# Dense feed-forward with 128-token blocks as the stationary operand of all three products, gate and up weights side by side, and the inner layer transposed on TensorE

## The chip, the cores and the metric

The program runs on one core of one Trainium2 chip. TensorE (PE) multiplies: a 128x128 stationary operand is loaded and up to 512 columns of the moving operand are streamed past it into a bank of PSUM. ScalarE (ACT), VectorE (DVE) and GpSimd (POOL) compute on data in SBUF, and ACT and DVE read PSUM too; SyncE (SP) issues the loads. The metric is the device time of one execution in microseconds.

## The reference

A ten-stage stack on 256 tokens of width 1024: mixers (latent attention and RWKV-7, Mamba-2, LRU with window attention, gated DeltaNet), two cross attentions, three dense feed-forward layers and one mixture of experts. The change touches the three dense layers. Each computes, with 2816 inner columns:

```python
def swiglu_ffn(h, norm, w13, w2):
    u = rms_norm(h, norm) @ w13
    return (jax.nn.silu(u[..., :FFN_HIDDEN]) * u[..., FFN_HIDDEN:]) @ w2
```

The third layer has gate, up and down weights as three tensors instead of two. The result is added to `h`. All inputs are float32.

## The kernel before, in words

The stages follow one another in one instruction program; `swiglu` writes the three dense stages ffn0, ffn1 and ffn2. Each engine has its own in-order program, and semaphores (`wait_ge`, `then_inc`) tie them. Every product is taken in three passes (`passes`, lines 194 to 196): each operand is a rounded high part and a remainder (low part), and high x high, low x high and high x low are added up in PSUM. ACT makes the high part of a weight by a cast, DVE the low part by a subtraction, and the low part is written over the raw weights in the ring.

The inner columns are worked off in 11 chunks of 256. A chunk's weights are 3 MB: gate (128 x 8 x 256 per partition view), up (the same) and down (128 x 2 x 1024); two buffers of 6144 columns, `units`, `low` and `high`, alternate. A chunk is two steps j of 128 inner columns, 22 steps in all.

- `up(i, first, j)` on PE: the weights are stationary (128 inner columns), the 256 tokens move. 2 (gate, up) x 8 (k) x 3 passes = 48 matmuls of 256 columns. The inner layer so comes out transposed, inner columns on partitions, as the down product needs it. Four banks, one for each step of two chunks.
- ACT applies Silu (L2102), DVE multiplies (L2133), ACT casts (L2104), DVE takes the remainder (L2135).
- `down(i, j)` on PE, two steps behind `up`: the transposed inner layer is stationary, 512 weight columns move. 2 (t) x 2 (n) x 3 passes = 12 matmuls of 512 columns into four banks `acc` that collect over the whole stage.

PE's order is up 0, up 1, up 2, down 0, up 3, down 1, and so on to up 21, down 19, down 20, down 21. SP loads gate and up of a chunk when the up steps of the chunk before the last are done (`up_columns`), and down when that buffer's down steps are done. ACT casts a chunk's gate and up (L2090) ahead of the Silu of the chunk before, and its down weights (L2108) after its own second step; DVE follows (L2118, L2138). The first and the last bodies of the loop are written out; the middle is a hardware loop over two chunks. In front of the stage the tokens are normalised and transposed (`norm_rows`, `transpose_split`, L355, L369, L382).

The expert stage, `experts_by_tile`, is not touched. In it 128 rows are stationary and 512 weight columns move in all three products (also in three passes), and its inner layer is turned on PE by four transposes (L2460) once per 72 matmuls.

## Time and profile before

| | |
|---|---|
| median of 3 runs | 3296.67 us |
| the runs | 3291.42, 3296.67, 3301.78 us |
| span of the profiled execution | 3301.1 us |
| PE / weight loads / DVE / ACT busy | 83% / 69% / 57% / 42% |
| ffn0 | first matmul of `up` 677.7, first of the four additions to `h` 871.8 us |
| ffn1 | 1288.6 to 1482.7 us |
| ffn2 | 1665.1 to 1858.6 us |

The profiled execution's own time beside its span is not listed apart; the highest of the three runs, 3301.78 us, lies 0.7 us over the span. Times of the trace are microseconds from the span's start. The three dense stages take some 194 us each, 18% of the span together.

### The profile page before, as it was taken

To read this page: it belongs to the slowest core of one execution; us is meant where nothing else is said; L and a number is where in the kernel's file an instruction comes from. 1 tells how busy PE (TensorE), PEld (TensorE's weight loads), DVE (VectorE), ACT (ScalarE), POOL (GpSimd) and SP (SyncE) were. 2 spreads that over 40 slices of the span, in tenths; PEclk is the share of its full clock that TensorE was granted. 3 is DMA by queue.
4 is the path that set the end of the run, shared out by engine and by line. 5 is a ranking of instruction groups with operands and counts; after the bars stand their busy time and mean duration, and the time that the engine had idled before them with its cause. 6 is when DMAs were issued, how large, how long until landed. Compare 5 with 4: busy or idle time off the path is not lost.

```text
span 3301.1 us, 38219 instructions
## 1 busy us (share of the span) xinstructions
PE 2755.3 (83%) x14374; PEld 2282.4 (69%) x14374; DVE 1880.5 (57%) x2337; ACT 1397.5 (42%) x1812; POOL 328.7 (10%) x197
## 2 busy tenths in 40 slices
PE   7036876789899877997889896757999999999999
PEld 6023765489787746985589785756877877877877
DVE  3054224354484524544354474347888888888887
ACT  3012111144353304432244351115776777777766
POOL 3020111000144400000000132220000000000000
PEclk9565777889897698998699897877999999999999
DMA  7330001055452113534055440006999999999996
GB/s 178 74 119 0 1 1 38 13 182 187 157 175 78 40 63 109 184 132 139 1 196 181 157 143 0 1 0 258 386 342 330 370 323 330 376 321 341 362 325 227
DMA packets 334486, 564.59 MB, mean 171 GB/s; under 512 B 60274, under 2 KB 139122, under 8 KB 334256
## 3 DMA queue, kind: packets, MB, share of 16 engines
q1 hardware_dynamic: 333552, 559.52, 48.5%
q0 software_dynamic: 544, 1.84, 0.2%
q8 instruction: 70, 1.15, 0.1%
q10 hardware_dynamic: 288, 1.83, 0.1%
q14 instruction: 32, 0.26, 0.0%
HBM read 560.27 MB, written 1.05 MB: 170 GB/s over the span
## 4 chain that ended last, share of the span: by engine, by line
PE 76%; DVE 10%; ACT 5%; SPq 3%; issue 2%; POOL 2%; DMA 1%; ACTq 0%; DVEq 0%; POOLq 0%
PE banks L194 18%; PE banks L196 17%; PE banks L195 17%; PE banks L452 5%; SPq L263 3%; PE banks L844 1%; PE banks L868 1%; PE banks L869 1%; POOL arena L393 1%; PE banks L2395 1%; DMA ring<-in_mla_w_uq 1%; PE banks L1771 1%; PE banks L704 1%; PE banks L2460 1%; ACT arena L854 1%
## 5 line engine op out<-in xcount | busy, mean ns | idle before, releaser
L2541 DVE TENSOR_TENSOR moe_weights_low<-ring,moe_weights_high 128x1024 fp32r<-128x1024 f32 x672 | 784.4, 1220 | 118.3 <-ACT moe_weights_high L2495 113.1
L2495 ACT CAST moe_weights_high<-ring 128x1024 fp32r<-128x1024 f32 x672 | 684.0, 1052 | 127.8 <-PE banks L196 123.1
L194 PE MATMUL banks<-moe_weights_high,moe_rows_high 128*128 128x512 f32 x896 | 357.6, 399 | 3.7 <-DVE moe_weights_low L2541 3.7
L196 PE MATMUL banks<-moe_weights_low,moe_rows_high 128*128 128x512 f32 x896 | 350.6, 391 | 0.0
L195 PE MATMUL banks<-moe_weights_high,moe_rows_low 128*128 128x512 f32 x896 | 349.9, 390 | 0.0
L194 PE MATMUL banks<-ffn_x_high,ffn_weights_high 128*128 128x256 f32 x1056 | 300.5, 285 | 15.4 <-DVE ring_low L2118 15.4
L195 PE MATMUL banks<-ffn_x_high,ring_low 128*128 128x256 f32 x1056 | 300.0, 284 | 0.0
L196 PE MATMUL banks<-ffn_x_low,ffn_weights_high 128*128 128x256 f32 x1056 | 299.5, 284 | 0.0
L2118 DVE TENSOR_TENSOR ring_low<-ring,ffn_weights_high 128x2048 fp32r<-128x2048 f32 x66 | 148.1, 2289 | 134.7 <-ACT ffn_weights_high L2090 134.7
L194 PEld LDWEIGHTS banks<-ffn_x_high,ffn_weights_high 128*128 128x128 f32 x1056 | 203.0, 192 | 18.9 <-issue 16.5
L195 PEld LDWEIGHTS banks<-ffn_x_high,ring_low 128*128 128x128 f32 x1056 | 202.3, 192 | 2.4
L196 PEld LDWEIGHTS banks<-ffn_x_low,ffn_weights_high 128*128 128x128 f32 x1056 | 202.7, 192 | 0.0
L194 PEld LDWEIGHTS banks<-moe_weights_high,moe_rows_high 128*128 128x128 f32 x896 | 169.0, 189 | 39.0 <-issue 5.5
L196 PEld LDWEIGHTS banks<-moe_weights_low,moe_rows_high 128*128 128x128 f32 x896 | 168.7, 188 | 36.2
L195 PEld LDWEIGHTS banks<-moe_weights_high,moe_rows_low 128*128 128x128 f32 x896 | 169.2, 189 | 35.5 <-issue 1.7
L487 POOL TENSOR_TENSOR ring_low<-ring,pieces_high 128x1024 fp32r<-128x1024 f32 (+2 forms) x63 | 169.0, 2695 | 219.0 <-ACT pieces_high L473 218.9
L194 PE MATMUL banks<-moe_weights_high,moe_hidden_high 128*128 128x512 f32 x448 | 176.7, 394 | 11.7 <-DVE moe_hidden_low L2553 11.7
L2090 ACT CAST ffn_weights_high<-ring 128x2048 fp32r<-128x2048 f32 x66 | 122.3, 1901 | 144.5 <-DMA ring<-in_ffn_w 64.8
L452 PE MATMUL banks<-ring,arena 128*128 128x512 f32 (+1 forms) x296 | 134.3, 615 | 52.7 <-DMA ring<-in_mla_w_uq 42.5
L196 PE MATMUL banks<-moe_weights_low,moe_hidden_high 128*128 128x512 f32 x448 | 174.6, 390 | 0.0
L195 PE MATMUL banks<-moe_weights_high,moe_hidden_low 128*128 128x512 f32 x448 | 174.4, 389 | 0.0
L393 POOL TENSOR_TENSOR arena<-arena,consts 128x2 f32<-128x2 f32 (+3 forms) x34 | 44.1, 1298 | 1115.6 <-DVE arena L414 786.0
(482 smaller groups left out, 5275.1 us busy)
## 6 DMA issues: line engine op xcount, KB each, us to landing
ring<-in_o_moe_w_gate SPq DMA_DIRECT2D x112, 1024.0 KB, 6.7
ring<-in_o_moe_w_up SPq DMA_DIRECT2D x112, 1024.0 KB, 7.3
ring<-in_o_moe_w_down SPq DMA_DIRECT2D x112, 1024.0 KB, 6.6
ring<-in_ffn_w SPq DMA_DIRECT2D x66, 1024.0 KB, 7.8
ring<-in_od_w_in SPq DMA_DIRECT2D x10, 2048.0 KB, 7.9
ring<-in_o_w_in SPq DMA_DIRECT2D x8, 2048.0 KB, 8.8
ring<-in_e_ffn_w_gate SPq DMA_DIRECT2D x11, 1024.0 KB, 5.4
ring<-in_e_ffn_w_up SPq DMA_DIRECT2D x11, 1024.0 KB, 7.9
```

Source lines behind the costliest of these rows:

```text
L194: pe.matmul(out_, lh, rh, start=start, stop=False)
L195: pe.matmul(out_, ll, rh, start=False, stop=False)
L196: return pe.matmul(out_, lh, rl, start=False, stop=stop)
L263: sp.dma_start(dst, src, allow_slow_non_contiguous=True).then_inc(self.sem, 16)
L393: pool.tensor_tensor(x, x, const("minus_half")[:, 0:n], ALU.pow).then_inc(*G.tick())
L452: last = pe.matmul(bank.ap[:, 0:n], lhs[0:rows, k, t * P:(t + 1) * P], view[:, k, :], start=(k == 0), stop=(k == n_k - 1))
L487: pool.tensor_tensor(low_view, view, high.bitcast(F32), ALU.subtract).then_inc(*G.tick())
L704: last = pe.matmul(bank.ap[:, t * T:(t + 1) * T], b["qk"][0:d, t * P:(t + 1) * P], b["qk"][0:d, T:2 * T], start=True, stop=True)
L2090: act.copy(high[b][:, c], units[b][:, c]).then_inc(up_high, 1)
L2118: dve.tensor_tensor(low[b][:, c], units[b][:, c], high[b][:, c].bitcast(F32), ALU.subtract).then_inc(up_low, 1)
L2495: act.copy(hi[:, b * 1024:(b + 1) * 1024], piece).then_inc(sems["hi_done"], 1)
L2541: dve.tensor_tensor(lo[:, b], piece, hi[:, b].bitcast(F32), ALU.subtract).then_inc(sems["lo_done"], 1)
```

## The change

The tokens become stationary in the gate and up products too. The gate and up weights of a chunk lie side by side, so that one matmul moves 512 columns (256 of gate, 256 of up): `up(i, first, b)` now does a whole chunk, 2 (token block t) x 8 (k) x 3 passes = 48 matmuls of 512 columns, in two banks. The inner layer then has tokens on partitions; `turn` transposes it by four 128x128 transposes into a third bank, ACT casts out of that bank (`hidden`, 512 wide) and DVE takes the remainder. `down(i, b)` does 24 matmuls of 512 columns, a chunk at a time and one chunk behind. The PE order is up 0, turn 0, up 1, down 0, turn 1, up 2, down 1, and so on to up 10, down 9, turn 10, down 10. SP loads down 0 ahead of gate and up of chunk 1. `transpose` is the same call that other stages use with `ident`.

```diff
             enter(stage)
-            sg = [room(T) for _ in range(4)]
-            hid = [room(T) for _ in range(4)]
-            hh, hl = ([split_room(f"{stage}_hidden{j}_{part}", T) for j in range(4)] for part in ("high", "low"))
+            FC = 2 * P
+            sg = [room(FC) for _ in range(TT)]
+            hid = [room(FC) for _ in range(TT)]
+            hh, hl = split_room(f"{stage}_hidden_high", TT * FC), split_room(f"{stage}_hidden_low", TT * FC)
             xh, xl = (split_room(f"{stage}_x_{part}", KD * T).rearrange("p (k t) -> p k t", t=T)
...
             normed = transpose_split(scaled, KD, scaled_ready, xh, xl, g, par.landed())
             high = [split_room(f"{stage}_weights{b}_high", UNIT) for b in range(2)]
...
-            up_banks, acc = banks[0:4], banks[4:8]
+            UP, HALF_UP = KD * 2 * FC, KD * FC
+            up_view = lambda u: u[:, 0:UP].rearrange("p (k n) -> p k n", n=2 * FC)
+            down_view = lambda u: u[:, UP:UNIT].rearrange("p (k n) -> p k n", n=D)
+            up_banks, turn_bank, acc = banks[0:2], banks[2], banks[4:8]
...
-                body(steps // 4, False, 2)
+                assert chunks % 2 == 1
+                body(0, True, 2)
+                with eng.Fori(1, chunks // 2) as i:
+                    body(i, False, 2)
+                body(chunks // 2, False, 1)
...
+                def load_up(b, c):
+                    w = up_view(units[b])
+                    sp.dma_start(w[:, :, 0:FC], src("gate", c).rearrange("(k p) n -> p k n", p=P)).then_inc(up_landed[b], 16)
+                    sp.dma_start(w[:, :, FC:2 * FC], src("up", c).rearrange("(k p) n -> p k n", p=P)).then_inc(up_landed[b], 16)
+
+                def load_down(b, c):
+                    sp.dma_start(down_view(units[b]), src("down", c).rearrange("(k p) n -> p k n", p=P)).then_inc(down_landed[b], 16)
...
+                def body(i, first, count):
+
+                    for b in range(count):
+                        c = i * (2 * FC) + b * FC
                         sp.wait_ge(up_done, i * 4 + (2 * b - 2))
-                    sp.dma_start(wg[b], src("gate", c).rearrange("(k p) n -> p k n", p=P)).then_inc(up_landed[b], 16)
-                    sp.dma_start(wu[b], src("up", c).rearrange("(k p) n -> p k n", p=P)).then_inc(up_landed[b], 16)
-
-                def body(i, first, count):
-                    for b in range(count // 2):
-                        if count == 4:
-                            up_columns(i + b, 1 - b)
-                        c = i * (4 * P) + b * (2 * P)
-                        if not first:
-                            sp.wait_ge(down_done, i * 4 + (2 * b - 2))
...
+                        load_up(b, c)
+                        if not (first and b == 0):
+                            sp.wait_ge(down_done, i * 2 + (b - 2))
+                        load_down(1 - b, c - FC)
+                load_up(0, 0)
+                load_down(0, 0)
+                load_up(1, FC)
+                body(1, True, 2)
+                with sp.Fori(2, chunks // 2) as i:
+                    body(i, False, 2)
+                body(chunks // 2, False, 1)
+                sp.wait_ge(down_done, chunks - 2)
+                load_down((chunks - 1) % 2, (chunks - 1) * FC)
...
-                def up(i, first, j):
-                    b = j // 2
-                    if not first:
-                        pe.wait_ge(product_done, i * 4 + (j - 3))
-                    ps = up_banks[j].ap
-                    for which, w in enumerate((gate_w, up_w)):
-                        if j % 2 == 0:
-                            pe.wait_ge(up_low, i * 4 + (j + which + 1))
+                def up(i, first, b):
+                    wh, wl = up_view(high[b]), up_view(low[b])
+                    for t in range(TT):
+                        if not (first and b == 0):
+                            pe.wait_ge(product_done, i * 4 + (2 * b + t - 1))
+                        tok = slice(t * P, (t + 1) * P)
                         for k in range(KD):
-                            c = slice((j % 2) * P, (j % 2 + 1) * P)
-                            wh, wl = w[b]
-                            last = passes(pe, ps[:, which * T:(which + 1) * T], (wh[:, k, c], wl[:, k, c]),
-                                          (xh[:, k, :], xl[:, k, :]), start=(k == 0), stop=(k == KD - 1))
-                    last.then_inc(up_done, 1)
...
-                            last = passes(pe, acc[t * 2 + n].ap, (hh[j][:, rows], hl[j][:, rows]),
-                                          tuple(w[:, j % 2, cols] for w in down_w[b]), start=start, stop=stop)
+                            if t == 0 and k % (KD // 2) == 0:
+                                pe.wait_ge(up_low, i * 4 + (2 * b + k // (KD // 2) + 1))
+                            last = passes(pe, up_banks[t].ap, (xh[:, k, tok], xl[:, k, tok]), (wh[:, k, :], wl[:, k, :]),
+                                          start=(k == 0), stop=(k == KD - 1))
+                        last.then_inc(up_done, 1)
+
+                def turn(i, b):
+
+                    pe.wait_ge(product_done, i * 4 + (2 * b + 2))
+                    for j in range(2):
+                        for t in range(TT):
+                            at = j * T + t * P
+                            last = pe.transpose(turn_bank.ap[:, at:at + P], hid[t][:, j * P:(j + 1) * P], ident)
+                    last.then_inc(turn_done, 1)
+
+                def down(i, b, start=False, stop=False):
+                    pe.wait_ge(down_low, i * 2 + (b + 1))
+                    pe.wait_ge(hl_done, i * 2 + (b + 1))
+                    wh, wl = down_view(high[b]), down_view(low[b])
+                    for j in range(2):
+                        for t in range(TT):
+                            rows = slice(j * T + t * P, j * T + (t + 1) * P)
+                            for n in range(2):
+                                cols = slice(n * 512, (n + 1) * 512)
+                                last = passes(pe, acc[t * 2 + n].ap, (hh[:, rows], hl[:, rows]), (wh[:, j, cols], wl[:, j, cols]),
+                                              start=start and j == 0, stop=stop and j == 1)
                     last.then_inc(down_done, 1)
 
...
+                    for b in range(count):
+                        before = (i, 0) if b else (i - 1, 1)
+                        if not (first and b == 0):
+                            turn(*before)
+                        up(i, first, b)
+                        if not (first and b == 0):
+                            down(*before, start=first)
                 run(body, pe)
-                down(steps // 4, 0)
-                down(steps // 4, 1, stop=True)
+                turn(chunks // 2, 0)
+                down(chunks // 2, 0, stop=True)
...
+                def up_part(i, b, n):
+
+                    if n == 0:
+                        act.wait_ge(up_landed[b], i * 32 + 32)
+                    c = slice(n * HALF_UP, (n + 1) * HALF_UP)
+                    act.copy(high[b][:, c], units[b][:, c]).then_inc(up_high, 1)
+
+                def silu(i, b, t):
+                    act.wait_ge(up_done, i * 4 + (2 * b + t + 1))
+                    act.activation(sg[t], up_banks[t].ap[:, 0:FC], ACT.Silu).then_inc(silu_done, 1)
+
+                def hidden(i, b):
+                    act.wait_ge(turn_done, i * 2 + (b + 1))
+                    act.copy(hh, turn_bank.ap).then_inc(hh_done, 1)
+
+                def down_part(i, b):
+                    act.wait_ge(down_landed[b], i * 16 + 16)
+                    act.copy(high[b][:, UP:UNIT], units[b][:, UP:UNIT]).then_inc(down_high, 1)
...
+                        up_part(0, 0, 0)
+                        up_part(0, 0, 1)
+                    for b in range(count):
+                        before, after = (i, 0) if b else (i - 1, 1), (i + 1, 0) if b else (i, 1)
+                        more = count == 2
+                        if not (first and b == 0):
+                            hidden(*before)
+                        if more:
+                            up_part(*after, 0)
+                        if not (first and b == 0):
+                            down_part(*before)
+                        silu(i, b, 0)
+                        if more:
+                            up_part(*after, 1)
+                        silu(i, b, 1)
                 run(body, act)
-
...
+                def product(i, b, t):
+                    dve.wait_ge(silu_done, i * 4 + (2 * b + t + 1))
+                    dve.tensor_tensor(hid[t], sg[t], up_banks[t].ap[:, FC:2 * FC], ALU.mult).then_inc(product_done, 1)
+
+                def hidden(i, b):
+                    dve.wait_ge(hh_done, i * 2 + (b + 1))
+                    dve.tensor_tensor(hl, turn_bank.ap, hh.bitcast(F32), ALU.subtract).then_inc(hl_done, 1)
+
...
-                dve.wait_ge(down_done, steps)
+                hidden(chunks // 2, 0)
+                down_part(chunks // 2, 0)
+                dve.wait_ge(down_done, chunks)
```

The rows below are from the instruction program of each engine. The first place is ACT in ffn0 where the stage begins, with the waits behind each row; before (L2090 casts gate and up, L2102 is Silu, L2104 casts the inner layer, L2108 casts down):

```order
L2102 ACT_TABLE_LOAD
L2102 ACTIVATE arena<-banks 128x256 [waits ffn0_up_done]
L2104 CAST ffn_hidden_high<-arena 128x256 [waits ffn0_product_done]
L2102 ACTIVATE arena<-banks 128x256 [waits ffn0_up_done]
L2104 CAST ffn_hidden_high<-arena 128x256 [waits ffn0_product_done]
L2108 CAST ffn_weights_high<-ring 128x2048 [waits ffn0_down0_landed]
L2090 CAST ffn_weights_high<-ring 128x2048 [waits ffn0_up_done,ffn0_up0_landed]
```

and after the change (L2105 casts half of gate and up, L2109 is Silu, L2113 casts the turned inner layer, L2117 casts down):

```order
L2109 ACT_TABLE_LOAD
L2109 ACTIVATE arena<-banks 128x256 [waits ffn0_up_done]
L2105 CAST ffn_weights_high<-ring 128x2048
L2109 ACTIVATE arena<-banks 128x256 [waits ffn0_up_done]
L2113 CAST ffn_hidden_high<-banks 128x512 [waits ffn0_turn_done]
L2105 CAST ffn_weights_high<-ring 128x2048 [waits ffn0_up0_landed]
L2117 CAST ffn_weights_high<-ring 128x2048 [waits ffn0_down0_landed]
L2109 ACTIVATE arena<-banks 128x256 [waits ffn0_up_done]
```

The cast of chunk 0's down weights now stands behind the first cast of chunk 2's gate and up, which waits for that chunk's load; before it stood ahead of it. The second place is PE in ffn0 from chunk 0 to chunk 1; before:

```order
L194 MATMUL banks<-ffn_x_high,ffn_weights_high 128x256
L195 MATMUL banks<-ffn_x_high,ring_low 128x256
L196 MATMUL banks<-ffn_x_low,ffn_weights_high 128x256
L194 MATMUL banks<-ffn_x_high,ffn_weights_high 128x256 [waits ffn0_up_low_done]
L195 MATMUL banks<-ffn_x_high,ring_low 128x256
L196 MATMUL banks<-ffn_x_low,ffn_weights_high 128x256
```

and after the change (L2070 is `turn`):

```order
L194 MATMUL banks<-ffn_weights_high,ffn_x_high 128x512
L195 MATMUL banks<-ffn_weights_high,ffn_x_low 128x512
L196 MATMUL banks<-ring_low,ffn_x_high 128x512
L2070 MATMUL banks<-consts,arena 128x128 [waits ffn0_product_done]
L2070 MATMUL banks<-consts,arena 128x128 x3
L194 MATMUL banks<-ffn_weights_high,ffn_x_high 128x512 [waits ffn0_up_low_done,ffn0_product_done]
L195 MATMUL banks<-ffn_weights_high,ffn_x_low 128x512
L196 MATMUL banks<-ring_low,ffn_x_high 128x512
```

Between the up products of chunk 0 and of chunk 1 there are now four transposes, which wait for the product on DVE. The third place is ACT in ffn0 at the stage's end, behind the loop; before:

```order
L2102 ACTIVATE arena<-banks 128x256 [waits ffn0_up_done]
L2104 CAST ffn_hidden_high<-arena 128x256 [waits ffn0_product_done]
L2102 ACTIVATE arena<-banks 128x256 [waits ffn0_up_done]
L2104 CAST ffn_hidden_high<-arena 128x256 [waits ffn0_product_done]
L2108 CAST ffn_weights_high<-ring 128x2048 [waits ffn0_down0_landed]
```

and after the change:

```order
L2113 CAST ffn_hidden_high<-banks 128x512 [waits ffn0_turn_done]
L2117 CAST ffn_weights_high<-ring 128x2048 [waits ffn0_down1_landed]
L2109 ACTIVATE arena<-banks 128x256 [waits ffn0_up_done] x2
L2113 CAST ffn_hidden_high<-banks 128x512 [waits ffn0_turn_done]
L2117 CAST ffn_weights_high<-ring 128x2048 [waits ffn0_down0_landed]
```

The down cast of the last chunk, L2117, now waits in line behind the cast of the turned inner layer.

## Rows read from the trace of the kernel before

**Rows 1.** The page: its head, and one group of part 5.

```profile
span 3301.1 us, 38219 instructions
...
L194 PE MATMUL banks<-ffn_x_high,ffn_weights_high 128*128 128x256 f32 x1056 | 300.5, 285 | 15.4 <-DVE ring_low L2118 15.4
```

**Rows 2.** Busy time by stretch, in the middle of ffn0.

```profile
core 0: us, PE busy (x) PEld busy (x) DVE busy (x) ACT busy (x) POOL busy (x), PEclk, DMA share, GB/s
...
709.00:726.00 17.00, 17.00 (x122) 15.90 (x122) 8.66 (x8) 8.23 (x8) 0.00 (x0) 1.00 0.55 188
```

**Rows 3.** Timeline of PE in ffn0: down 18, up 21, down 19.

```profile
850.20 0.40 PE L194 MATMUL banks<-ffn_weights_high,ffn_hidden_high 128*128 128x512 f32 x1
...
853.00 0.28 PE L194 MATMUL banks<-ffn_x_high,ffn_weights_high 128*128 128x256 f32 x1
...
858.67 0.40 PE L194 MATMUL banks<-ffn_weights_high,ffn_hidden_high 128*128 128x512 f32 x1
```

**Rows 4.** Timeline of SP in ffn0: gate loads of neighbouring chunks.

```profile
757.25 0.37 SPq L2024 DMA_DIRECT2D ring<-in_ffn_w  x1
...
774.23 0.37 SPq L2024 DMA_DIRECT2D ring<-in_ffn_w  x1
```

**Rows 5.** Timeline of PE in the expert stage, from transposes to transposes.

```profile
2831.89 0.60 PE L2460 MATMUL banks<-consts,arena 128*128 128x128 f32 x4
...
2832.79 0.40 PE L196 MATMUL banks<-moe_weights_low,moe_rows_high 128*128 128x512 f32 x1
...
2834.87 0.39 PE L196 MATMUL banks<-moe_weights_low,moe_rows_high 128*128 128x512 f32 x1
...
2843.71 0.39 PE L196 MATMUL banks<-moe_weights_low,moe_rows_high 128*128 128x512 f32 x1
...
2848.70 0.60 PE L2460 MATMUL banks<-consts,arena 128*128 128x128 f32 x4
```

**Rows 6.** The chain in the expert stage: start, length, what; four transposes.

```profile
2815.25 0.44 PE banks L2460 x4
```

**Rows 7.** Timelines of SP and ACT: chunk 2's load and first cast.

```profile
691.98 0.37 SPq L2024 DMA_DIRECT2D ring<-in_ffn_w  x1
...
700.38 1.90 ACT L2090 CAST ffn_weights_high<-ring 128x2048 fp32r<-128x2048 f32 x1 [5.30 <-DMA ring<-in_ffn_w]
...
1678.91 0.37 SPq L2024 DMA_DIRECT2D ring<-in_e_ffn_w_gate  x1
...
1688.77 3.71 ACT L2090 CAST ffn_weights_high<-ring 128x2048 fp32r<-128x2048 f32 x2 [6.77 <-DMA ring<-in_e_ffn_w_up]
```

**Rows 8.** Timelines of ACT and DVE: two casts and their two remainders.

```profile
748.64 3.71 ACT L2090 CAST ffn_weights_high<-ring 128x2048 fp32r<-128x2048 f32 x2 [5.39 <-PE banks L196]
...
750.57 4.49 DVE L2118 TENSOR_TENSOR ring_low<-ring,ffn_weights_high 128x2048 fp32r<-128x2048 f32 x2 [5.00 <-ACT ffn_weights_high L2090]
```

**Rows 9.** The chain at the end of ffn0: start, length, what.

```profile
858.88 0.39 ACT arena L2102
...
859.29 0.43 DVE arena L2133
...
860.06 1.91 ACT ffn_weights_high L2108
...
861.99 2.30 DVE ring_low L2138
...
864.34 0.68 PE banks L194
```

**Rows 10.** Busy time by stretch: stage start, after the last stall.

```profile
682.00:684.00 2.00, 2.00 (x13) 2.00 (x12) 2.00 (x2) 0.79 (x1) 0.00 (x0) 0.60 0.00 0
...
865.00:866.00 1.00, 1.00 (x4) 0.80 (x3) 0.00 (x0) 0.00 (x0) 0.00 (x0) 0.50 0.00 0
...
868.00:869.00 1.00, 1.00 (x6) 0.80 (x5) 0.00 (x0) 0.00 (x0) 0.00 (x0) 1.00 0.00 0
```

**Rows 11.** Groups by form: the 512-wide cast out of PSUM.

```profile
L2507 ACT CAST moe_hidden_high<-banks 128x512 fp32r<-128x512 f32 x56 | 33.0, 589 | 16.8 <-PE banks L2460 16.8
```

More of the change, by code:

```diff
@@ L1968, in memory_once, with swiglu @@
             return transpose_tiles(mem, KD, V.at(), memT)
[L1971 removed]
+        def swiglu(stage, gain, src, n_chunks):
             par = Params(stage)
@@ L1987, in swiglu @@
             high = [split_room(f"{stage}_weights{b}_high", UNIT) for b in range(2)]
-            steps = 2 * n_pairs
+            chunks = n_chunks
             up_landed = [new_semaphore(f"{stage}_up{b}_landed") for b in range(2)]
             down_landed = [new_semaphore(f"{stage}_down{b}_landed") for b in range(2)]
-            up_done, silu_done, product_done, hh_done, hl_done, down_done = (
-                new_semaphore(f"{stage}_{n}_done") for n in ("up", "silu", "product", "hidden_high", "hidden_low", "down"))
+            up_done, silu_done, product_done, turn_done, hh_done, hl_done, down_done = (
+                new_semaphore(f"{stage}_{n}_done")
+                for n in ("up", "silu", "product", "turn", "hidden_high", "hidden_low", "down"))
             up_high, up_low, down_high, down_low = (
@@ L2068, in down @@
                     last.then_inc(down_done, 1)
                 def body(i, first, count):
-                    for j in range(count):
-                        up(i, first, j)
-                        if j >= 2:
-                            down(i, j - 2, start=(first and j == 2))
-                        elif not first:
-                            down(i - 1, j + 2)
+                    for b in range(count):
[5 more added lines that the diff above has]
+                            down(*before, start=first)
@@ L2121, in body @@
                 def body(i, first, count):
                     if first:
[L2123 to L2139 removed]
+                        up_part(0, 0, 0)
@@ new lines, in body @@
+                        up_part(0, 0, 1)
+                    for b in range(count):
+                        before, after = (i, 0) if b else (i - 1, 1), (i + 1, 0) if b else (i, 1)
+                        more = count == 2
+                        if not (first and b == 0):
+                            hidden(*before)
+                        if more:
+                            up_part(*after, 0)
+                        if not (first and b == 0):
+                            down_part(*before)
+                        product(i, b, 0)
+                        if more:
+                            up_part(*after, 1)
+                        product(i, b, 1)
@@ L2148, in swiglu @@
             for s in slots:
-                s.free = (down_done, steps)
+                s.free = (down_done, chunks)
         def experts_by_tile():
```

78 lines of the change are left out of this document (11 added, 67 removed).

## Prediction

> **What bounds the kernel now.** I read the page first [rows 1]: TensorE is the busiest engine, and the matmuls of the gate and up products waited 15.4 us in all three dense stages together, all of it for the first weights of a stage. Then I looked at the busy time by stretch in the middle of ffn0 [rows 2]: in 17 us PE is busy for 17.00, at a granted clock of 1.00 (the 2.4 GHz level), while DVE has 8.66, ACT 8.23 and the DMA engines 0.55. So the body of a dense stage is bound by PE alone, and what it costs is the distance between matmuls, not the length that a record shows (285 ns for 256 columns in [rows 1], though the next one starts after less than half of it). The reader is to take distances from starts. In [rows 3] step 18's down takes 853.00 - 850.20 = 2.80 us for 12 matmuls of 512 columns, 0.2333 us each, and step 21's up 858.67 - 853.00 = 5.67 us for 48 matmuls of 256 columns, 0.118 us each. Per column the two are nearly the same (0.456 and 0.461 ns). A chunk is two such pairs, 16.94 us by these starts; the loads of two neighbouring chunks are 774.23 - 757.25 = 16.98 us apart [rows 4]. I take 16.96.
>
> Last I read the two ends of a stage in the chain [rows 9], where PE does wait: after the last up step ACT casts the last down weights, DVE takes the remainder, and PE goes on at 864.34.
>
> **The change, part by part.**
>
> *Up product.* 96 matmuls of 256 columns become 48 of 512: the same 24,576 columns. At the distance of the present down product that is 48 x 0.2333 = 11.2 us for 11.34. The stage nearest to the new form is the expert stage, where 128 rows are stationary, 512 weight columns move, and four transposes come after every 72 matmuls, exactly the new chunk. [Rows 5] give its cycle: 2848.70 - 2831.89 = 16.81 us. Within it the first matmuls behind the transposes are (2834.87 - 2832.79) / 9 = 0.231 us apart, the later ones (2843.71 - 2834.87) / 39 = 0.2267.
>
> *Transposes.* Four per chunk, 44 more per stage. They stand on PE's path, with nothing to hide them: 0.44 us for four [rows 6], which is inside the 16.81.
>
> The new chunk by this is 16.81 us against 16.96: -0.15, times 11 chunks = **-1.7 us per stage**. Bounds: all 72 at 0.2333 plus 0.44 makes 17.24, +3.1 per stage; all at 0.2267 plus 0.44 makes 16.76, -2.2. I take the expert stage's cycle, since it has the same operands, the same count and the same turn.
>
> A fixed cost per matmul would speak for the change. The Trainium skill (TensorE: Matmul & The Clock Gate, the section on 56 against 53.3 ns) gives a warm distance of N/2.4 plus some 2.5 ns, 109.2 and 215.8 ns; the trace's 118 and 227 to 233 lie above both, and by the page alone the 48 matmuls fewer would save 0.12 us a chunk. The same page (Part 4: PE-mode transpose) puts a transpose at about 275 ns in a kernel; the trace's four in 0.44 us are 110 ns each, and by the page the 33 turns would cost 33 x (1.10 - 0.44) = 22 us more than I sum.
>
> *ACT and DVE in the loop.* The 256-wide casts and remainders of the inner layer become one 512-wide each; their sum hardly moves and both engines are half idle. The order matters more. Count from the end of up(c-1), which releases the load of chunk c+1. From that load's issue to the first cast are 700.38 - 691.98 = 8.4 us [rows 7]. Two casts take 3.71, and two remainders, which start 1.93 behind the casts, 4.49 [rows 8]. Behind the first half of gate and up of chunk c+1 now stand the down weights of c-1: ready at 8.4 + 1.9 + 4.5 = 14.8. PE meanwhile does down(c-2), the turn and up(c): 5.5 + 0.4 + 10.9 = 16.8. Hidden, with 2.0 us to spare.
>
> *Head of the stage.* In the first chunk there is no down product to cover anything. PE ends up(0) and at once wants turn(0), which waits for Silu and product: 0.39 + 0.43 and handovers, up to 859.29 + 0.43 - 858.88 = 0.84 by [rows 9], **+0.95** with PE's own start. Before, four banks let PE go straight on. Then up(1) ends at 0.95 + 0.44 + 10.9 = 12.3 after up(0), but chunk 0's down weights, queued on ACT and DVE behind the cast that waits for chunk 2's load, are ready only at 14.8: **+2.5 us** of waiting ahead of down(0). In ffn2 the same load took 1688.77 - 1678.91 = 9.9 us [rows 7], so there it is +4.0. Behind this PE instruction stands all of the stage. Bounds: 2.0 if the load comes half a microsecond sooner, 4.0.
>
> After a wait of about 2.8 us at the end of ffn0 (from 858.67 [rows 3] + 12 x 0.2333 = 861.5 to 864.3 [rows 9]) the granted clock was 0.50, the 1.2 GHz level, and 1.00 again from 868 [rows 10]: some 9 matmuls at 0.43 for 0.23, 1.8 us. The wait of 2.5 us is a little shorter; I take **+1.7**, and 0 as the lower bound.
>
> *Tail of the stage.* Before, the last down cast ran under down(19), and PE stood still for 2.8 us. Now PE does down(9), turn(10), and only then may ACT cast the inner layer (0.59 [rows 11]) and behind it, in ACT's order, the last down weights. From the transposes' last start-to-start distance: 0.60 - 0.44 = 0.16 for their records to end [rows 5, 6], 0.59 for the cast, then 1.9 and 2.3 [rows 9], 5.0 in all: **+2.2 us**. A longer stop may mean a longer slow stretch afterwards (at the stage's start the clock was still at 0.60 in 682 to 684, six microseconds after the first matmul [rows 10]): **+0.7**, between 0 and 1.5.
>
> *At nothing:* the loads (same bytes, same 1 KB rows), the start of the stage (the first half of the weights still has 2048 columns), and the two PSUM banks for four (the product that frees a bank comes more than 4 us ahead of its next use).
>
> **Sum.** Per stage -1.7 + 0.95 + 2.5 + 1.7 + 2.2 + 0.7 = +6.35; three stages and 1.5 more for ffn2: +20.5 us. The profiled execution has a span of 3301.1, 4.4 over the median of the runs; 3301.1 + 20.5 = 3321.6 there, and 3317 against the median 3296.67. About 0.3% (10 us) is what a measurement of this kernel can tell from no change.
>
> **Rivals.**
> - *Same, at some +8 to +12 us (0.17).* The clock holds through the short wait and is no slower after the tail: 20.5 - 3 x 2.4 = +13; with the cycle at 16.76 it is +12, and with the load half a microsecond sooner +10. For it: the head wait is shorter than the one in the rows. Against: the tail stop is longer than it. 3307 us.
> - *The distance stays 0.2333 (0.17).* In the dense stages PE reads the same buffers as today's down product, and today's 0.2333 is theirs. Cycle 17.24: 33 x 0.43 = 14 us more, +35, 3332 us.
> - *A turn or a late remainder costs in every chunk (0.08).* Either the transposes are dearer among rounded matmuls, or the 2.0 us of slack are not there. The price is whatever is late, 30 times or more: one microsecond is 30 us, +50 in all, 3347 us. The 0.44 us of [rows 6] and a load of 8.4 us against an allowed 10.4 speak against it; ffn2's 9.9 would leave 0.5. The Trainium skill's 275 ns a transpose (same page and part) would make it +42.
> - *Faster (0.03).* The distance of 512-wide matmuls falls so far that it pays for both ends. The ends cost 25.6 us, 0.78 a chunk; so 72 distances must fit in 16.96 - 0.44 - 0.78 = 15.74, 0.2187 us each. The floor is 512 columns at 2.4 GHz, 0.2133 us: 33 x (15.80 - 16.96) + 25.6 = -13 us, 3284 us. No row shows a distance under 0.2267. The Trainium skill's rule above (0.2158) would give 33 x (15.98 - 16.96) + 25.6 = -7 us.
>
> The likeliest case holds 0.55, with a range of its own of 3309 to 3325. The range of 3303 to 3334 takes in the first rival and most of the second. Slower: 0.55 + 0.17 + 0.08 = 0.80; within 0.3%: 0.17; faster: 0.03.
>
> **What the profile after would show.** Right: 512-wide up matmuls 0.227 to 0.231 us apart; four transposes in 0.44 us; a cycle near 16.8 us with PE never waiting in it; in each stage one wait of about 1 us ahead of the first turn, one of 2.5 to 4 us ahead of the first down for the remainder of its weights, with the clock at 0.50 behind it; 5 us without matmuls before the last down. Each dense stage some 6 to 8 us longer. Wrong: a cycle over 17.1 or under 16.6, down weights ready before up(1) ends, or waits of PE in every chunk. The forecast fails most easily by the granted clock behind the two waits, which I know from one length of wait only.

## The result

| | before | after |
|---|---|---|
| median | 3296.96 us (4 runs) | 3335.94 us (4 runs, 3333.48 to 3341.7) |
| span of the profiled execution | 3301.1 us | 3339.9 us |
| ffn0, first matmul to first addition to `h` | 194.1 us | 207.3 us |
| ffn1 | 194.1 us | 204.2 us |
| ffn2 | 193.6 us | 206.8 us |

The changed kernel is slower: ratio 1.0113, 95% interval 1.0094 to 1.0131, 39 us. Slower was forecast, at +20.5 us with a range up to 3334; the time lies just above the range. The three dense stages have grown from 581.8 to 618.3 us, 36.5 us of the 38.8 by which the two spans differ; the rest of the program takes 2.3 us more in this execution.

The page after, its head and the group of the gate and up product (DVE's L2159 is the remainder of the down weights):

```profile
span 3339.9 us, 35134 instructions
...
L194 PE MATMUL banks<-ffn_weights_high,ffn_x_high 128*128 128x512 f32 x528 | 216.1, 409 | 15.4 <-DVE ring_low L2146 15.4
```

and, from the groups by line and form, the down product:

```profile
L194 PE MATMUL banks<-ffn_weights_high,ffn_hidden_high 128*128 128x512 f32 x264 | 110.7, 420 | 23.6 <-DVE ring_low L2159 23.6
```

The gate and up product has 528 matmuls in a group where it had 1056 [rows 1], and its only long wait is still the one for a stage's first weights, 15.4 us. The down product now waits 23.6 us in all. Who waits for whom, PE only (us in total, times, longest); before, the down product waited in the tails alone:

```profile
PE banks L194 <- DVE ring_low L2138: 8.1, 3, 2.7
```

and after the change:

```profile
PE banks L194 <- DVE ring_low L2159: 23.6, 6, 4.8
...
PE banks L194 <- DVE ring_low L2146: 15.4, 3, 5.1
```

Six waits, two in each stage: that is the head and the tail of the forecast. The head of ffn0, in the timelines of SP (the load of chunk 2), ACT, DVE and PE:

```profile
689.70 0.37 SPq L2021 DMA_DIRECT2D ring<-in_ffn_w  x1
```

```profile
699.52 1.90 ACT L2105 CAST ffn_weights_high<-ring 128x2048 fp32r<-128x2048 f32 x1 [7.63 <-DMA ring<-in_ffn_w]
701.33 1.90 ACT L2117 CAST ffn_weights_high<-ring 128x2048 fp32r<-128x2048 f32 x1
```

```profile
701.45 2.29 DVE L2146 TENSOR_TENSOR ring_low<-ring,ffn_weights_high 128x2048 fp32r<-128x2048 f32 x1 [8.84 <-ACT ffn_weights_high L2105]
703.66 2.28 DVE L2159 TENSOR_TENSOR ring_low<-ring,ffn_weights_high 128x2048 fp32r<-128x2048 f32 x1
```

```profile
690.60 0.66 PE L2070 MATMUL banks<-consts,arena 128*128 128x128 f32 x4 [0.93 <-DVE arena L2151]
...
706.00 0.79 PE L194 MATMUL banks<-ffn_weights_high,ffn_hidden_high 128*128 128x512 f32 x1 [3.54 <-DVE ring_low L2159]
...
714.47 0.60 PE L2070 MATMUL banks<-consts,arena 128*128 128x128 f32 x4
```

The load issued at 689.70 lets ACT begin at 699.52; the cast of the down weights stands behind it, its remainder starts at 703.66, and PE, which came out of up(1) 3.54 us earlier, goes on at 706.00. The 0.93 us ahead of the first transposes is the uncovered Silu and product. Busy time by stretch behind the wait (the column behind POOL is the granted clock):

```profile
706.00:707.00 1.00, 1.00 (x2) 0.83 (x3) 1.00 (x2) 0.00 (x0) 0.00 (x0) 0.50 1.09 358
710.00:711.00 1.00, 1.00 (x4) 0.80 (x3) 0.00 (x0) 0.00 (x0) 0.00 (x0) 0.50 0.03 8
711.00:712.00 1.00, 1.00 (x4) 0.81 (x3) 0.00 (x0) 0.00 (x0) 0.00 (x0) 0.50 0.00 0
```

Five to six microseconds after PE goes on the clock still stands at 0.50, the 1.2 GHz level. The tail of ffn0, in the chain:

```profile
869.81 0.45 PE banks L2070 x4
...
870.77 1.91 ACT ffn_weights_high L2117
872.70 2.30 DVE ring_low L2159
875.05 0.80 PE banks L194
...
878.83 0.43 PE banks L196
...
883.51 1.89 DVE h L2186 x3
```

This is the row-by-row answer to [rows 9]: transposes, the cast of the last down weights behind that of the inner layer, the remainder, and PE again at 875.05, 4.8 us after the transposes, with 0.43 us a matmul until 879.6.

The body of the stage is where the forecast fails. PE never waits there, but the transposes stand at

```profile
869.65 0.60 PE L2070 MATMUL banks<-consts,arena 128*128 128x128 f32 x4
```

and at 714.47 above, nine chunks apart: 155.18 / 9 = 17.24 us a chunk, and not 16.81 as in [rows 5]. The matmuls in one of them:

```profile
767.10 0.40 PE L196 MATMUL banks<-ring_low,ffn_x_high 128*128 128x512 f32 x1
...
777.60 0.40 PE L196 MATMUL banks<-ring_low,ffn_x_high 128*128 128x512 f32 x1
...
783.20 0.39 PE L196 MATMUL banks<-ring_low,ffn_hidden_high 128*128 128x512 f32 x1
```

(777.60 - 767.10) / 45 = 0.2333 us, and (783.20 - 777.60) / 24 = 0.2333: the 512-wide up matmuls have the distance of the down matmuls of [rows 3], to the last digit. Work of the other engines beside them is not the reason. At the end of the stage nothing else runs, and the distance is (882.01 - 879.91) / 9 = 0.2333 us there too; the first two lines are the timeline, the third is busy time by stretch:

```profile
879.91 0.40 PE L194 MATMUL banks<-ffn_weights_high,ffn_hidden_high 128*128 128x512 f32 x1
...
882.01 0.40 PE L194 MATMUL banks<-ffn_weights_high,ffn_hidden_high 128*128 128x512 f32 x1
```

```profile
880.00:882.00 2.00, 2.00 (x10) 1.60 (x9) 0.00 (x0) 0.00 (x0) 0.00 (x0) 1.00 0.00 0
```

### The profile page after: what moved, and what is told of

The parts are those of the page before. It is cut to its first block, busy times and chain, and to the rows that moved or that the text cites. A ratio compares the mean times of both kernels' runs of the same rounds, so it can differ in the third digit from the quotient of the medians.

```text
span 3339.9 us, 35134 instructions
## 1 busy us (share of the span) xinstructions
PE 2776.4 (83%) x12922; PEld 2224.6 (67%) x12922; DVE 1874.8 (56%) x2304; ACT 1389.9 (42%) x1779; POOL 329.1 (10%) x197
## 4 chain that ended last, share of the span: by engine, by line
PE 75%; DVE 10%; ACT 5%; SPq 3%; issue 2%; DMA 2%; POOL 2%; ACTq 0%; DVEq 0%; POOLq 0%
PE banks L194 17%; PE banks L196 17%; PE banks L195 17%; PE banks L452 5%; SPq L263 3%; PE banks L844 1%; PE banks L868 1%; PE banks L869 1%; POOL arena L393 1%; DMA ring<-in_mla_w_uq 1%; PE banks L2437 1%; PE banks L1771 1%; PE banks L704 1%; PE banks L2502 1%; ACT arena L854 1%
## 5 line engine op out<-in xcount | busy, mean ns | idle before, releaser
L194 PE MATMUL banks<-ffn_weights_high,ffn_x_high 128*128 128x512 f32 x528 | 216.1, 409 | 15.4 <-DVE ring_low L2146 15.4
L196 PE MATMUL banks<-ring_low,ffn_x_high 128*128 128x512 f32 x528 | 211.5, 400 | 0.0
L195 PE MATMUL banks<-ffn_weights_high,ffn_x_low 128*128 128x512 f32 x528 | 210.7, 399 | 0.0
L2105 ACT CAST ffn_weights_high<-ring 128x2048 fp32r<-128x2048 f32 x66 | 125.1, 1901 | 70.7 <-DMA ring<-in_ffn_w 45.2
L473 ACT CAST pieces_high<-ring 128x1024 fp32r<-128x1024 f32 (+2 forms) x126 | 125.8, 1033 | 55.0 <-PE banks L196 55.0
L452 PEld LDWEIGHTS banks<-ring,arena 128*128 128x128 f32 x296 | 59.1, 202 | 125.1 <-issue 114.1
L481 DVE TENSOR_TENSOR ring_low<-ring,pieces_high 128x1024 fp32r<-128x1024 f32 (+2 forms) x63 | 117.9, 1886 | 34.6 <-ACT pieces_high L473 34.5
```

The source lines that it names most:

```text
L194: pe.matmul(out_, lh, rh, start=start, stop=False)
L195: pe.matmul(out_, ll, rh, start=False, stop=False)
L196: return pe.matmul(out_, lh, rl, start=False, stop=stop)
L452: last = pe.matmul(bank.ap[:, 0:n], lhs[0:rows, k, t * P:(t + 1) * P], view[:, k, :], start=(k == 0), stop=(k == n_k - 1))
L473: act.copy(high, view).then_inc(*S.tick())
L481: dve.tensor_tensor(low_view, view, high.bitcast(F32), ALU.subtract).then_inc(*V.tick())
```

## The experiments

The open question was why the same form of matmul goes at 0.2267 us in the expert stage and at 0.2333 in a dense stage, and whether the ends cost what I had said. Each run is set beside the kernel before on the same chip; that kernel's median was 3297 to 3303 us on them, so microseconds against the changed kernel, which was timed apart from them, are rougher than the ratios. A cycle is the time from one turn's transposes to the next.

### First: where the operands begin, how PE is fed, and the transposes

A look at the memory of the two stages shows one difference, in where the operands begin within a partition (the byte address that the program gives them, and of it the remainder on division by 512). In the expert stage all operands begin at 128 modulo 512 bytes. In the dense stages tokens and inner layer begin at 384, the high weights at 416 and the low weights, in the ring, at 288: both kinds of weights lie 32 bytes off a multiple of 64. The other difference is in PE's program: the expert stage waits and signals every six matmuls.

**The high weights moved by 32 bytes.**

```diff
+            top[0] = -(-top[0] // 16) * 16
             high = [split_room(f"{stage}_weights{b}_high", UNIT) for b in range(2)]
```

> The changed kernel with the high weights of the dense stages (the moving operand of two of three passes) moved up by 32 bytes, so that they begin at a multiple of 64 bytes, as all operands of the expert stage do. Theory A (the 0.2333 us between 512-wide matmuls comes from a moving operand that begins 32 bytes off a multiple of 64): two of three distances fall to 0.227, three matmuls take 0.687 instead of 0.70 us, the cycle falls from 17.24 to 16.9 us, the program by some 10 us against the changed kernel (ratio to before near 1.008). Theory B (it comes from how often PE's program waits and signals, every six matmuls in the expert stage): cycle 17.24, ratio 1.011 as without it.

Measured: ratio 1.0083 (1.0062 to 1.0105), 3329.0 us. The transposes are here:

```profile
717.32 0.60 PE L2071 MATMUL banks<-consts,arena 128*128 128x128 f32 x4
...
870.62 0.60 PE L2071 MATMUL banks<-consts,arena 128*128 128x128 f32 x4
```

(870.62 - 717.32) / 9 = 17.03 us. The distance moved with an address alone; but all three distances fell, to some 0.230, and not two of three to 0.227. Theory A lives, its detail does not.

**The ring moved too.** `pad_ring = sb("pad_ring", 8)` ahead of the ring and 8 columns more ahead of the arena.

> As the run with the high weights moved, and the ring too, in which the raw and the low weights of all stages lie. Theory A: all three distances 0.227 in the dense stages, cycle 16.8 us, some 14 us less than the changed kernel in these stages (ratio to before near 1.007), and the 0.231 us of the stages that take weights from the ring in pieces may fall too. Theory B: cycle 17.24, ratio 1.011.

Measured: ratio 1.0092 (1.0073 to 1.0112), 3331.8 us; nine cycles from 715.61 to 869.60, 17.11 us. By the cycle this is worse than one move alone; the ratios of the two runs can't be told apart. The padding had also moved the tokens, to 448 modulo 512, with the high weights at 0 and the ring at 320: the operands lay farther apart than before. So a multiple of 64 is not what counts. In this run the expert stage lies at 192 modulo 512 with all its operands, and its cycle is still 16.80 us, (2639.63 - 2606.04) / 2:

```profile
2606.04 0.60 PE L2505 MATMUL banks<-consts,arena 128*128 128x128 f32 x4
...
2639.63 0.60 PE L2505 MATMUL banks<-consts,arena 128*128 128x128 f32 x4
```

**The feed of PE.** A wait ahead of every sixth up matmul and a signal behind it:

```diff
+                            if k % 2 == 0:
+                                pe.wait_ge(up_low, i * 4 + (2 * b + (2 if t else k // (KD // 2) + 1)))
                             last = passes(pe, up_banks[t].ap, (xh[:, k, tok], xl[:, k, tok]), (wh[:, k, :], wl[:, k, :]),
                                           start=(k == 0), stop=(k == KD - 1))
+                            if k % 2 == 1 and k < KD - 1:
+                                last.then_inc(six_done, 1)
```

> The changed kernel with a wait ahead of every sixth matmul of the up product (on a count that is already there) and a signal behind every sixth, as the expert stage has them. Theory B: distances in up fall to 0.227, cycle 16.9. Theory A: 0.2333 stays, cycle 17.24, perhaps a little more for the signals.

Measured: ratio 1.0113 (1.0094 to 1.0132); nine cycles of 17.24 us:

```profile
716.39 0.60 PE L2073 MATMUL banks<-consts,arena 128*128 128x128 f32 x4
...
871.58 0.60 PE L2073 MATMUL banks<-consts,arena 128*128 128x128 f32 x4
```

Theory B falls.

**One transpose of four.** In `turn`, `range(1)` for both loops; the output is not the reference's.

> The changed kernel with one of the four transposes per chunk; the other three quarters of the turned inner layer are left out (old contents of the bank are used), so that the output is not the reference's. If the four cost their 0.44 us and nothing around them, the cycle falls by three quarters of it to 16.9 us and the program by 33 x 0.33 = 11 us, ratio 1.008. If a turn also slows what stands behind it, the cycle falls by more (16.7 or less); if it overlaps with something, by less.

Measured: ratio 1.0089 (1.0068 to 1.0109); nine cycles of 16.91 us:

```profile
717.05 0.27 PE L2070 MATMUL banks<-consts,arena 128*128 128x128 f32 x1
...
869.21 0.27 PE L2070 MATMUL banks<-consts,arena 128*128 128x128 f32 x1
```

Three transposes are worth 0.33 us a chunk, 0.11 each. They cost what [rows 6] say, and 72 x 0.2333 + 0.44 = 17.24 leaves nothing around them. One record is longer than that; the groups by form of the changed kernel give 273 ns:

```profile
L2070 PE MATMUL banks<-consts,arena 128*128 128x128 f32 x132 | 19.9, 273 | 2.8 <-DVE arena L2151 2.8
```

The Trainium skill (TensorE: Matmul & The Clock Gate, Part 4: PE-mode transpose) gives about 275 ns for one in a kernel; the trace agrees with it as the length of a record. What a transpose adds to PE's path is the distance between starts, and the prediction's rival took the length for it.

### Second: all operands at multiples of 128, the counter-test, and the ends

**All at multiples of 128.**

```diff
+        SMALL = 1560
+        small = sb("small_tensors", SMALL)
         ring_base = nc.sbuf_base
...
+            top[0] = -(-top[0] // 32) * 32
             high = [split_room(f"{stage}_weights{b}_high", UNIT) for b in range(2)]
```

> The changed kernel with the small tensors put ahead of the ring and the high weights of the dense stages 96 bytes further on, so that ring, low weights, high weights, tokens and inner layer of these stages all begin at multiples of 128 bytes, like all operands of the expert stage. Theory A, mended (the distance between 512-wide matmuls follows from where the operands begin, modulo 128 bytes; moving one of them gave 17.03 us, moving all by odd amounts 17.1): cycle 16.80 us as in the expert stage, 33 x 0.44 = 14.5 us less than the changed kernel, ratio to before 1.007. Theory C (it is something else about the dense stages, and the two shifted runs differ by chance of another kind): cycle between 17.0 and 17.24, ratio 1.009 to 1.012.

Measured: ratio 1.0099 (1.0078 to 1.0121), 3330.6 us; nine cycles from 713.72 to 866.18, 16.94 us. By averages over the starts of 120 us, two of the three distances are 0.228, the one from the second to the third pass is 0.232. The cycle 16.80 that the mended theory A expected did not come, so a multiple of 128 is not enough: the tokens and the ring lay at 384 modulo 512, the high weights at 0.

**The same in the kernel before.**

> The same two moves of memory in the kernel before. Theory A: its down distance falls from 0.2333 to 0.227 (0.15 us a chunk); its up distance of 0.118 for 256 columns may fall too; cycle 16.96 to 16.8 or lower, ratio 0.998 or lower. Theory C: cycle 16.96, ratio 1.000.

Measured: ratio 0.9995 (0.9984 to 1.0006), 3299.2 us. Its loads of chunks are 757.01, 773.88, 790.72, 807.59 and 824.42, 16.85 us apart for 16.96; the dense stages together take 578.7 us for 581.8. Theory A expected a cycle of 16.8 or lower and a ratio of 0.998 or lower; a gain of 3 us is below what the runs can tell.

**The counter-test in the expert stage,** where everything is alike: its high and low weights 32 bytes on.

```diff
+            top[0] = -(-top[0] // 32) * 32 + 8
             hi, lo = split_room("moe_weights_high", NB * 1024), split_room("moe_weights_low", NB * 1024)
+            top[0] += 24
```

> The changed kernel with the high and low weights of the expert stage (the moving operands) 32 bytes further on, so that they lie to a multiple of 128 bytes as the dense stages' do; nothing else moves against 128. Theory A: the expert stage's cycle of 72 matmuls rises from 16.80 to 17.24 us, 0.44 in each of 56 cycles, 25 us in all, ratio to before near 1.019. Theory C: 16.80 stays, ratio 1.0115.

Measured: ratio 1.0203 (1.0180 to 1.0225), 3364.0 us, 28 us over the changed kernel by the medians. Transposes of the expert stage (L2504 here; its `pe.transpose` is at L2460 in the kernel before):

```profile
2600.11 0.60 PE L2504 MATMUL banks<-consts,arena 128*128 128x128 f32 x4
...
2617.41 0.60 PE L2504 MATMUL banks<-consts,arena 128*128 128x128 f32 x4
```

17.30 us where [rows 5] have 16.81, and distances of 0.234; over 56 cycles that is 27 us. The weights now lie at 160 modulo 512. The 24 columns behind them moved the rows and the inner layer as well, from 128 to 256, so this run alone does not part the place of the moving operand against the stationary one from either place by itself. It does show that addresses alone make the distance in a stage that the change did not touch.

**The ends.** On ACT and DVE alike:

```diff
                         if not (first and b == 0):
                             hidden(*before)
+                        if first and b == 1:
+                            down_part(*before)
                         if more:
                             up_part(*after, 0)
-                        if not (first and b == 0):
+                        if not first:
                             down_part(*before)
...
-                hidden(chunks // 2, 0)
                 down_part(chunks // 2, 0)
+                hidden(chunks // 2, 0)
```

> The changed kernel with two changes of order on ACT and DVE: the first chunk's down weights are split ahead of the first half of chunk 2's gate and up, and the last chunk's down weights ahead of its turned inner layer. If the prediction's account of the ends is right, the wait ahead of the first down product (3.5 us in ffn0) and the slow clock behind it go, and the wait ahead of the last falls from 4.8 to some 1.5 us with no slow clock behind it: 17 us from the heads and some 15 from the tails of three stages, ratio to before near 1.002. If the waits only move, the gain is under 10 us and the ratio over 1.009.

Measured: ratio 1.0004 (0.9992 to 1.0015), 3301.6 us, 34 us under the changed kernel by the medians; the dense stages together take 585.9 us for 618.3. Who waits for whom on PE, in the stretch of ffn0:

```profile
PE banks L194 <- DVE ffn_hidden_low L2157: 1.5, 1, 1.5
PE banks L2070 <- DVE arena L2153: 0.9, 1, 0.9
```

No wait for down weights is left; 1.5 us for the turned inner layer at the end and the 0.9 us ahead of the first turn are. Busy time behind the last wait:

```profile
868.00:870.00 2.00, 1.57 (x7) 1.33 (x8) 0.29 (x1) 0.00 (x0) 0.00 (x0) 1.00 0.00 0
870.00:872.00 2.00, 2.00 (x10) 1.60 (x9) 0.00 (x0) 0.00 (x0) 0.00 (x0) 1.00 0.00 0
```

The clock stays at 1.00 after 1.5 us. In ffn1 and ffn2 the same wait is 1.49 us, and the clock stays at 1.00 too.

### Third: alike modulo 512, the head alone, and the two causes together

**All at 384 modulo 512.** As the run at multiples of 128, but `top[0] = -(-top[0] // 128) * 128`.

> The changed kernel with all matmul operands of the dense stages beginning at the same offset modulo 512 bytes (384), as those of the expert stage do (128 there). In the run at multiples of 128 the high weights lay at 0 and all else at 384, and one of three distances stayed at 0.232 (cycle 16.94). Theory A2 (what counts is that the three operands lie alike, modulo 512): all distances 0.227, cycle 16.80, ratio 1.007. Theory A1 (it is modulo 128 and the rest is something else): cycle 16.94 as before, ratio 1.0085 to 1.010.

Measured: ratio 1.0077 (1.0061 to 1.0092), 3324.4 us. Transposes:

```profile
714.73 0.60 PE L2071 MATMUL banks<-consts,arena 128*128 128x128 f32 x4
...
865.96 0.60 PE L2071 MATMUL banks<-consts,arena 128*128 128x128 f32 x4
```

(865.96 - 714.73) / 9 = 16.80 us: the expert stage's cycle, and the forecast's.

**The kernel before in that memory.**

> The kernel before in the same memory. Theory A2: down distance 0.227, and its up distance perhaps lower too, cycle 16.8 or less, ratio 0.9975 or less. Theory A1: as at multiples of 128, ratio 0.9995.

Measured: ratio 0.9996 (0.9987 to 1.0006). Its chunk loads from 739.74 to 824.72 are 17.00 us apart, no less than the 16.96 of before. Theory A2 expected a down distance of 0.227 and a cycle of 16.8 or less, and was wrong for this kernel. Its down distances fall to 0.229, as they did with the high weights at 0; its 256-wide up distances rise from 0.118 to 0.120. So the rule that fits the long rows of 512-wide matmuls does not carry over to matmuls of 256 columns with the weights stationary, nor in full to runs of twelve 512-wide ones between them; what does was not looked for.

**The head alone.**

> The changed kernel with only the first chunk's down weights split ahead of the first half of chunk 2's gate and up. The heads of the three stages took 17 us over three plain cycles, so the time falls by 17 us, ratio 1.0065; the tails stay as they are.

Measured: ratio 1.0070 (1.0055 to 1.0085), 3321.7 us: 14 us under the changed kernel. The dense stages together fall from 618.3 to 601.5 us, 16.8, where 17 was expected; the tails' three waits of 4.8 us are still there.

**Ends and memory together.**

> The same memory together with both changes of order at the ends. The two causes are in different places and should add: against the kernel before, the ends alone gave 1.0004; a cycle of 16.80 takes 14.5 us more, ratio 0.996; with the cycle at 16.94, 0.9975.

Measured: 3292.6 us, ratio 0.9984 (0.9975 to 0.9993), 11 runs. The dense stages together take 570.9 us for 581.8 before. The two causes add there (618.3 - 32.4 for the ends is 585.9, measured; 15.0 less for the memory). The program as a whole missed its expectation of 0.996: it gained 5.9 us by its medians, and not the 11 of these stages. The spans of the two profiled executions do differ by 11.4 us (3301.1 and 3289.7), but that of the kernel before is one execution, the longest of its four.

**Alike, but off a multiple of 128.** The ring stays where it was, at 288 modulo 512; `top[0] += 104` ahead of the inner layer and `top[0] = -(-(top[0] - 104) // 128) * 128 + 104` ahead of the high weights put the rest there.

> The changed kernel with the ring where it was (288 modulo 512 bytes, 32 modulo 128) and the inner layer, the tokens and the high weights of the dense stages moved to 288 modulo 512 as well. Likeness alone (what counts is that the operands begin alike modulo 512): all distances 0.227, cycle 16.80 us, ratio 1.0075. Likeness and a multiple of 128: distances over 0.23, cycle 17.0 to 17.24, ratio 1.009 to 1.012.

Measured: ratio 1.0069 (1.0053 to 1.0085), 3324.9 us. Transposes:

```profile
718.25 0.60 PE L2072 MATMUL banks<-consts,arena 128*128 128x128 f32 x4
...
869.55 0.60 PE L2072 MATMUL banks<-consts,arena 128*128 128x128 f32 x4
```

(869.55 - 718.25) / 9 = 16.81 us. The ring was not moved here. Likeness is enough; no multiple of 128 is needed.

> The same with both changes of order at the ends. Likeness alone: 14.5 us under the run with the ends alone (ratio 1.0004), 0.996, and not over the 0.9984 of the run with all at 384; otherwise 0.998 to 1.0005.

Measured: 3295.0 us, ratio 0.9986 (0.9976 to 0.9995), dense stages together 571.3 us. By the ratio this misses the 0.996 of likeness and falls where the other case was put; the cycle, 16.81 us, and the stages, 14.6 us under the run on the ends, are those of likeness. The ratio of the whole program can't settle it, since it came out between the two for the memory at 384 as well.

| kernel | tokens, high, low modulo 512 | cycle | dense stages |
|---|---|---|---|
| changed | 384, 416, 288 | 17.24 us | 618.3 us |
| align_both | 448, 0, 320 | 17.11 | 612.2 |
| align_high | 384, 448, 288 | 17.03 | 612.5 |
| all128 | 384, 0, 384 | 16.94 | 607.6 |
| equal512 | 384, 384, 384 | 16.80 | 606.5 |
| equal288 | 288, 288, 288 | 16.81 | 603.2 |

The cycle is shortest where all three are alike, but it does not grow in step with how far apart they begin. The stages of equal512 and equal288 differ by 3.3 us at one and the same cycle: so much do the ends of the stages differ from one execution to another.

## Why the prediction was wrong

The direction was right, and so were most parts; one term of the sum was mis-sized, and it had the wrong sign. Against the spans, +20.5 us was forecast and +38.8 measured.

- **The step that failed: "I take the expert stage's cycle, since it has the same operands, the same count and the same turn."** It was -0.15 us a chunk, -5.1 in all; measured was +0.28, +9.3 in all, which is 14.4 of the 18.3 us missing. The count and the turn were the same, the operands were not: they begin at other addresses. The second rival, "the distance stays 0.2333", with its cycle of 17.24 and +35 us, was the case that came true, and I gave it 0.17. Its reason, "the same buffers as today's down product", was nearer to the cause than mine. When the operands are put alike, the forecast's 16.80 appears. The step took a distance over from another stage without comparing addresses, and against the dense stage's own 0.2333 in [rows 3].
- **The up product itself.** Half as many matmuls of twice the columns were 48 x 0.2333 = 11.2 us for 11.34, as worked out from the down product. The gain of the change is this 0.14 us a chunk.
- **Transposes.** 0.44 us for four, right; shown by the run with one. The prices of 22 us and +42 that the prediction worked out from 275 ns took the length of a record for a distance.
- **ACT and DVE in the loop.** No wait of PE in any chunk but the first and the last, as forecast.
- **Head.** The two waits are there. Turn 0 to turn 1 takes 23.87, 21.10 and 23.78 us for a cycle of 17.24: 6.6, 3.9 and 6.5 us, 17.0 in all, where the parts (waits and slow clock) made 14.1. The load in ffn0 took 9.8 us and not 8.4, so that the wait is 3.54 us and not 2.5; but ffn2 has 3.69 for 4.0 and ffn1 1.99 for 2.5, and the three waits make 9.2 us for 9.0. What is left of the 17.0, 7.8 us, is the slow clock, for which 5.1 stood in the sum: it is the second term that was too small. It came after the shortest of the three waits too. With the order repaired the 17 us went.
- **Tail.** 4.8 us of waiting for 5.0, in all three stages. Waiting and clock together cost 7.4 us over the kernel before (27.2 - 17.0 - 2.8, the last for the waits ahead of the first turn), for 8.7.
- **Ends together.** 36.5 - 9.3 = 27.2 us for the 25.6 of the forecast. Two misses in it go opposite ways, 2.7 us more for the slow clock in the heads and 1.3 less for the tails, so that the nearness is in part luck. Some 2.3 us of the difference of the spans lie outside the dense stages and have no cause that was looked for; the runs of one kernel differ by more.
- **At nothing:** the loads in the loop, the start of the stage (15.4 us of waiting before and after) and the two banks cost nothing, as said.

What remains open: why likeness of the start addresses matters, whether 512 bytes is the period (operands 256 bytes apart were not tried), why the 256-wide matmuls do not follow it, and how much of the 10 to 11 us that the dense stages of the best two kernels gain in their traces is there in every execution, since the medians show 3 to 6. The kernel before, put at 384, took 579.1 us in its dense stages with a cycle of 17.00 and 581.8 in its own memory with 16.96, so a single trace of these stages is good to some 3 us.

## What to carry to other kernels

A distance between matmuls read from another stage is a row for the new one only if the operands lie alike too: compare start addresses, or take the distance from the stage that is changed, and give the other as the bound. A chunk loop that gives up a second set of banks or a second step of lead pays at its two ends, where no product covers the chain of casts; count that chain, and put what waits for no load ahead of what does in an engine's order. Both are a few lines to mend: here they turned a loss of 39 us into a gain of 3 to 6 by the medians.

## What the runs showed of the hardware

- For 512-wide matmuls of rounded float32, each with its own weight load, the distance at a granted clock of 1.00 is 0.227 us when stationary and moving operands begin alike modulo 512 bytes (at 128, 192, 288 or 384), and up to 0.234 when they do not: 72 of them and four transposes take 16.80 to 17.30 us. The first nine or so behind the transposes are 0.229 to 0.232 apart also where all is alike. The columns alone are 512 / 2.4 GHz = 0.2133. The Trainium skill (SBUF — State Buffer, Operand start alignment) asks that an operand start at a multiple of its element size, as a rule of legality and not of speed. All of these do, and their distances differ all the same.
- A wait of PE of 1.99 us was followed by a granted clock of 0.50; one of 1.5 us, in the run on the ends, was not. The first stands in the head of ffn1 of the changed kernel, busy time by stretch:

```profile
1328.00:1330.00 2.00, 1.02 (x4) 0.86 (x5) 2.00 (x3) 0.55 (x2) 0.00 (x0) 0.99 0.87 251
1330.00:1332.00 2.00, 2.00 (x6) 1.54 (x5) 1.79 (x2) 0.00 (x0) 0.00 (x0) 0.50 1.09 365
...
1334.00:1336.00 2.00, 2.00 (x10) 1.59 (x9) 0.00 (x0) 0.00 (x0) 0.00 (x0) 1.00 0.26 83
```

PE is busy for 1.02 of the first two microseconds, the next two are at 0.50, and from 1334 on the clock stands at 1.00 again. So the clock fell here when PE had already been at work again for about a microsecond.
- Four fp32 transposes of 128x128 behind matmuls take 0.44 us of PE's path, and three of them 0.33, though each record is 0.27 us long.
